# Hybrid decoder step: attention loop written out, second branch's inputs loaded early, first norm and first feed-forward tile reordered

## What is computed

```python
u_a = (jax.nn.silu(rg) * rn) @ w_pa
u_b = fox_o.reshape(b, t, FOX_W) @ w_pb
merged = jax.nn.sigmoid(ga) * u_a + jax.nn.sigmoid(gb) * u_b
mix = merged @ w_o
...
h = layer_norm(ALPHA * x + mix, ln1_w, ln1_b)
u, g = h @ w_up, h @ w_gate                    # D_FF = 2816
a = gelu(causal_conv3(u) + conv_b) * g
y = layer_norm(ALPHA * h + a @ w_down, ln2_w, ln2_b)
```

## Time and profile before

| | us |
|---|---|
| runs shown | 2134.36, 2138.0, 2139.96; median 2138.0 |
| profiled execution | 2139.22, of which the span between first and last instruction is 2137.5 |
| TensorE busy | 1989.5 (93% of the span) |
| VectorE, ScalarE, GpSimd busy | 1159.1, 648.8, 218.8 |
| granted TensorE clock | 0.97 on average |

### The profile page before, as it was taken

How to read it: one execution, slowest core, us unless ns; L and a number is a source line. 1 busy time by engine, 2 the same in 40 slices (tenths; PEclk the granted TensorE clock), 3 DMA queues, 4 the chain that set the end, 5 groups by cost and what they waited for, 6 DMA issues and landing times.

```text
span 2137.5 us, 39105 instructions
## 1 busy us (share of the span) xinstructions
PE 1989.5 (93%) x14335; PEld 1861.5 (87%) x14335; DVE 1159.1 (54%) x1771; ACT 648.8 (30%) x1179; POOL 218.8 (10%) x253
## 2 busy tenths in 40 slices
PE   7898998899999899989898898799999999999996
PEld 5796896798898798878798897799999999999996
DVE  4554454977867867885424856533322333233348
ACT  4444343134133223213401103434301322132224
POOL 1000000020020020020000101300000000100004
PEclk9999999999999999989999999899999999999999
DMA  4211101787987878886732310111111111111144
GB/s 126 63 32 50 40 21 51 233 311 245 310 281 262 301 264 298 278 308 231 252 94 89 106 49 11 40 49 40 50 49 50 40 48 43 54 42 49 43 142 131
DMA packets 151682, 276.50 MB, mean 129 GB/s; under 512 B 19042, under 2 KB 57951, under 8 KB 151543
## 3 DMA queue, kind: packets, MB, share of 16 engines
...
q0 software_dynamic: 23232, 82.80, 13.0%
...
## 4 chain that ended last, share of the span: by engine, by line
PE 44%; DVE 5%; DMA 1%; issue 1%; ACT 1%; SPq 0%; DVEq 0%; ACTq 0%
PE bank L121 40%; PE bank L1670 3%; DVE x_lo L1898 1%; DMA gated_raw<-gated_t_scratch 1%; DVE chunk_tmp L1827 1%; DVE chunk_tmp L1829 0%; DVE z L1895 0%; DVE moving_lo L1833 0%; DVE merged_hi L1831 0%; PE banks L1628 0%; DVE w_lo L1968 0%; DMA tail_raw<-in_w_down_dram 0%; DVE y L1944 0%; DMA z<-fox_t_scratch 0%; PE banks L1656 0%
## 5 line engine op out<-in xcount | busy, mean ns | idle before, releaser
L121 PE MATMUL bank<-x_hi,w_hi 128*128 128x344 f32 (+1 forms) x1944 | 641.5, 330 | 44.4 <-DVE x_lo L1898 15.1
L121 PE MATMUL bank<-x_lo,w_hi 128*128 128x344 f32 (+1 forms) x1944 | 631.6, 325 | 0.0
L121 PE MATMUL bank<-x_hi,w_lo 128*128 128x344 f32 (+1 forms) x1944 | 631.3, 325 | 0.0
L121 PEld LDWEIGHTS bank<-x_hi,w_hi 128*128 128x128 f32 (+1 forms) x1944 | 372.4, 192 | 61.6 <-issue 48.6
L121 PEld LDWEIGHTS bank<-x_lo,w_hi 128*128 128x128 f32 (+1 forms) x1944 | 372.5, 192 | 1.6
L121 PEld LDWEIGHTS bank<-x_hi,w_lo 128*128 128x128 f32 (+1 forms) x1944 | 372.1, 191 | 1.7
L97 ACT ACTIVATE w_hi<-w_raw 128x1024 fp32r<-128x1024 f32 (+3 forms) x139 | 142.1, 1022 | 453.7 <-PE bank L121 419.5
L121 PE MATMUL bank<-moving_hi,w_hi 128*128 128x344 f32 x744 | 227.0, 327 | 13.7 <-DVE moving_hi L1806 7.0
L121 PE MATMUL bank<-moving_lo,w_hi 128*128 128x344 f32 x744 | 237.6, 319 | 0.0
L104 DVE TENSOR_TENSOR w_lo<-w_raw,w_hi 128x1024 fp32r<-128x1024 f32 (+3 forms) x139 | 164.4, 1182 | 103.2 <-ACT w_hi L97 101.4
L121 PE MATMUL bank<-moving_hi,w_lo 128*128 128x344 f32 x648 | 208.1, 321 | 0.0
...
## 6 DMA issues: line engine op xcount, KB each, us to landing
...
```

What stands on the lines that cost most here:

```text
L121: mm = pe.matmul(g.bank[n][0:m, 0:TC], w[slot][:, k, 0:m], x[:, k, chunk(n)], start=(k == 0 and i == 0), stop=(k == kt - 1 and i == 2))
```

## The change

Three things are changed.

**Attention loop.** On all five engines the loop of two in `fox` is written out as straight code.

```diff
             @block.tensor
             def _(pe):
-                with pe.Fori(0, NIT) as it:
+                for it in range(NIT):
                     for u in range(2):
```

```diff
-        raw = [g_raw[:, n, :] for n in range(KD)] + [z[:, KB + n, :] for n in range(KB)]
+        fo_slot = [z[:, KB + n, :] for n in range(KB)]
+        raw = [g_raw[:, n, :] for n in range(KD)] + [gate[0][:], gate[1][:], stage[0][:, 0:T], fo_slot[3]]
...
+                for b in (0, 1):
+                    for n in range(NCH):
+                        sp.wait_ge(g.bank_free[n], JA + KD - 1 - b + 1)
+                    load_raw(KD + b)
+                load_raw(KD + 2)
                 sp.wait_ge(g.mm_chunk, NCH * (RING + JB))
-                for n in range(KD, KD + KB):
-                    load_raw(n)
+                load_raw(KD + 3)
                 for i in range(KD, 2 * KD):
+                    if i < KD + 2:
+                        sp.wait_ge(s_lo, i + 1)
                     load_gate(i)
...
                 split_hi(g, act, job(JB, JB % 2, 0), KB)
+                act.wait_ge(g.mm_chunk, NCH * (RING + JB))
                 for n in range(KD, KD + KB):
                     raw_hi(n)
...
-                dve.memset(zsum[:], 0.0).then_inc(z_part, 1)
...
                 merged(LAST, 1)
+                dve.memset(zsum[:], 0.0).then_inc(z_part, 1)
                 dve.wait_ge(s_lo, KD + KB)
```

```diff
+                        up_and_gate(1, f0, ju)
                         for k in range(NCH):
-                            pool.wait_ge(normed, (k + 1) * KD)
+                            pool.wait_ge(h_full, (k + 1) * KD)
+                            pool.wait_ge(h_lo, (k + 1) * KD)
                             for t in range(KD):
-                                ins = pool.tensor_scalar(acc[:, t, chunk(k)], z[:, t, chunk(k)], ln_cols[:, 1, t:t + 1], ALPHA, ALU.add, ALU.mult)
+                                ins = pool.tensor_scalar(acc[:, t, chunk(k)], z[:, t, chunk(k)], ALPHA, None, ALU.mult)
...
+                pe.wait_ge(centred, NCH)
+                pe.wait_ge(root, 2)
+                for n in range(NCH):
+                    for (j, slot), dst in ((up_job, bank[n]), (gate_job, gate_bank[n])):
+                        pe.wait_ge(g.w_split, RING + j + 1)
+                        pe.wait_ge(g.bank_free[n], ju + 1)
+                        for k in range(KD):
+                            pe.wait_ge(h_lo, n * KD + k + 1)
+                            for q, (w, x) in enumerate(((g.w_hi, g.xh), (g.w_hi, g.xl), (g.w_lo, g.xh))):
+                                mm = pe.matmul(dst[:, 0:TC], w[slot][:, k, :], x[:, k, chunk(n)],
+                                               start=(k == 0 and q == 0), stop=(k == KD - 1 and q == 2))
+                        mm.then_inc(g.mm_chunk, 1)
+                pe.wait_ge(z_part, 2)
+                pe.wait_ge(g.bank_free[NCH - 1], ju + 2)
+                pe.transpose(bank[3][0:NS + 2, 0:P], up[:, SEQ:SEQ + NS + 2], g.ident[:]).then_inc(cr_t, 1)
...
+                    with pe.Fori(0 if f0 else 1, n) as i:
+                        product(g, pe, job(i * 2 + ju, ju % 2, 0), g.xh, g.xl)
                         product(g, pe, job(i * 2 + ju, ju % 2, 1), g.xh, g.xl)
...
+                        act.activation(z[:, k, chunk(n)], z[:, k, chunk(n)], ACT.Identity, scale=ln_cols[:, 0, k:k + 1], bias=ln_cols[:, 1, k:k + 1]).then_inc(h_full, 1)
+                        act.wait_ge(h_full, n * KD + k + 1)
+                        act.activation(g.xh[:, k, chunk(n)], z[:, k, chunk(n)], ACT.Copy).then_inc(h_hi, 1)
                 act.wait_ge(ln_land, 32)
                 squares(0)
+                split_hi(g, act, job(JF, JF % 2, 1))
                 squares(1, range(0, 3))
...
+                        if first:
+                            act.wait_ge(g.mm_chunk, NCH * (RING + ju) + 2 * NCH - 1)
                         split_hi(g, act, job(i * 2 + ju, ju % 2, 2))
...
+                    if s == 0:
+                        tile(0, True)
+                    with act.Fori(1 if s == 0 else 0, n) as i:
+                        tile(i, False)
...
+                centre(0)
+                split_lo(g, dve, job(JF, JF % 2, 1))
+                centre(1)
+                centre(2)
+                dve.memset(up[:, 0:2], 0.0).then_inc(z_part, 1)
...
+                invert(0)
+                for k in range(KD):
+                    scale(0, k)
+                for n in range(NCH):
+                    if n < NCH - 1:
+                        invert(n + 1)
                     for k in range(KD):
+                        h_low(n, k)
+                        if n < NCH - 1:
+                            scale(n + 1, k)
...
+                            if first:
+                                dve.wait_ge(g.mm_chunk, NCH * (RING + ju) + 2 * k + 2)
+                            else:
+                                chunk_ready(g, dve, i * 2 + ju + 1, k)
```

56 lines of the change are left out of this document (30 added, 26 removed).

## The result

The changed kernel takes 2113.28 us (median of 4 runs, 2112.10 to 2114.90), the kernel before beside it 2138.98. The ratio is 0.9884, with a 95% interval of 0.9869 to 0.9900: 24.8 us less (21.4 to 28.0). A second set of runs gave 0.9891 (0.9873 to 0.9909). The forecast was 19.0 us less, 2119, in a range of 2112 to 2127. So the time lies in the range, near its lower end, and the direction is right; but 19.0 lies outside the interval of the measured gain, and some 4 to 6 us were not in the sum. The profiled execution took 2114.34 us with a span of 2112.4; the spans differ by 25.1 us.

The account below looks back on a forecast made before the run. TensorE, busy for 93% of the span, was taken as the bound, so time could come only from its standstills or lower clock. 7.5 + 4.5 + 7.0 = 19.0 us less than 2138.0 gave 2119, range 2112 to 2127.

Parts of the forecast that it names:

- Part A: Attention loop written out: TensorE's stall at the loop's jump and the half clock behind it go; 7.5 us, 4.3 to 9.5.
- The term for the rest: Attention: registers that computed semaphore values go too, in engines handing over work in softmax steps; 0.5 us, bounded 0 to 1.5.
- Part B: Raw inputs of the JB jobs: three loads come early, so merging starts sooner after the JA jobs; 4.5 us, 3.3 to 4.9.
- Part C: Norm and feed-forward tile 0: a loss at the start, a gain at the end, tile 1 starting earlier; 7.0 us, 1.0 to 9.
- The split's loss: Norm's start: VectorE stops behind the first centring for tile 0's gate weights, so ScalarE starts `h_high` 4.1 us late.
- The middle: Norm's 24 tiles, now two ScalarE passes each, 1.10 us a tile; it ends 1.8 us later than before.
- give-backs: Before tile 1: GpSimd's `acc` chunk beside the convolution costs 1.1 us, TensorE's possible start at the lower clock 1.0.
- the third rival: All three changed places reach the good ends of their bounds: 23.4 us less, 2114.6; chance 0.12 with beyond.
- The first rival: Norm: ScalarE's second pass becomes the bound, `x_lo` ends some 6 us later, 2125; chance 0.18.
- the second (a wait that remains): Attention: the 5.16 us idle time remains, so writing out the loop gives 0 to 1 us, 2126; chance 0.08.
- the fourth (straight code starves TensorE): Attention: fetching falls behind once in each pair, four stalls make 25 us, 2145, slower; chance 0.03.
- The fifth: ScalarE's second pass bounds the norm and the attention loop gives nothing, together: 2132; chance 0.03.

Follow-up runs that it names:

- the old arithmetic: Changed kernel with the norm's former arithmetic: one ScalarE pass for the high half, weight and bias on VectorE; median 2114.07 us, ratio 0.9890 to the kernel before.

## Why the prediction was right, and where it was short

**Part A: the mechanism right, two terms too small.** The forecast was 7.5 us (4.3 to 9.5); over all traces the stage takes 239.8 us with all loops and 229.8 without, 10.0 less, outside that range. That the 5.16 us were TensorE's own jump is shown: the idle time was there, 5.26 us, with every other engine written out, and went with TensorE's loop alone. That the sequencer fetches code in this time is the reading of the prediction; the row says only issue. The term for the jump was 7.0, chosen between the idle time and the pairs' difference of 8.0; pair 2 fell by 8.2. The term for the rest was 0.5, for registers, but pair 3 fell from 77.1 to 75.2, which I had taken for its plain length. With all loops the half clock in the softmax of pairs 2 and 3 was longer, which I had not priced. By the pairs above, 3.4 us of it in each pair are worth 2 to 3 us, most of the 3.7 that went with the other engines' loops. This part of the cause is argued from the traces and not isolated.

One row was misread, without harm: the 0.11 us of the earlier trace rows between two feed-forward tiles is the transpose of L1644, and TensorE has no idle time there. So the short loop's jump costs nothing that can be seen. And retention does have a standstill that is put down to issue, the one of 3.1 us in the earlier trace rows, so straight code is not free of them; it is there in all fourteen traces (2.1 to 3.5 us) and changes nothing in the comparison.

The Trainium skill, "Runtime: NRT & Kernel Launch", section Instruction fetch mechanics, says that a taken branch out of the fetched window stalls; this case's rows agree, with 4.6 to 5.5 us of idle time in the five traces with TensorE's loop, and none behind the short loop's jump. In the first trace the idle time above the usual 0.7 is 4.5 of the 10.0 us.

**Part B: right, and a little too small.** Merging starts 7.2 to 7.3 us after the JA jobs in seven of the nine traces with this part and 6.8 in the other two, where it was 12.0: 4.8 us earlier, or 5.2, for a forecast 4.9. Over all traces the stage is 159.4 us without and 154.0 with the part: 5.3, above the range's 4.9. I had taken off 0.4 for chunks at the lower clock, whatever the old kernel did there. But the old kernel had the half clock at the start of merging too (0.59), and its stretch, by the stretch view, was over 10 us long against 3.4 or 6.8. Where it is 3.4, the stage takes 153.1 to 153.7 us (four traces), where it is 6.8, 154.2 to 154.9 (the other five): so the clock gave something back instead of taking it. (The bound of 1.6 us for what could come back is not what its own numbers give, two chunks at 3.4 - 2.3 = 1.1 each, so 2.2; nothing hung on it.)

**Part C: right, with errors that cancel.** The forecast was 7.0, the stage gave 6.8 in the first pair of traces and 7.2 over all. The split's loss was to be 4.1 us; 3.9 was read, and 4.2 came back when it was moved. The period of ScalarE was 1.09 us for a forecast 1.10. The middle ended 1.3 us later for a forecast 1.8. From the last low half to tile 1 it took 8.2 us instead of 17.9 (the 18.1 of the working had the old start 0.2 late); forecast 7.2 and up to two give-backs. These were sized wrong one by one: GpSimd beside the convolution cost 0.6 us and not 1.1 (from the convolution's first step to the first gate product 4.7 us, in the next tile 4.1); the last up chunk is copied 1.1 us behind the last low half and not 0.5, because TensorE was still busy with the products before it; and the start of tile 1 at the lower clock cost 1.6, not 1.0. VectorE's row of the convolution beside GpSimd, which takes 1.28 us in the next tile:

```profile
1343.37 1.52 DVE L1967 SCALAR_TENSOR_TENSOR stage<-stage,conv_cols_tile 128x1024 f32<-128x1024 f32 x1 [2.64 <-ACT stage L1783]
```

The Trainium skill's rule of a locked port pair ("SBUF — State Buffer", section SBUF: two separate sides), which I had weighed at 4 us, did not hold as a full lock in these rows: VectorE's low halves went from 0.52 to 0.78 us in seven of 24, GpSimd's instructions took 1.14 us (median) instead of 0.80 (their form had changed too), and three of the convolution's four steps grew by 0.2 us each.

**What was in no term.** 4.7 us of retention and 2.9 us lost at the start. The second is scatter. Of the first, the means over all traces leave 3.6 us that may belong to the change, and that stays open.

**How much was luck.** The measured time is the one of the third rival (23.4 us less, 2114.6), to which I gave 0.12 with all beyond, and not the forecast's own 2119. The three stages give 10.0 + 5.3 + 7.2 = 22.5 us, which would be 2115.5. So the range would have held by the three parts alone. But parts A and B both lie above their own bounds, and part C is not at its upper end, as that rival had it: the time came out there for other reasons than the rival's.

The first rival (ScalarE's second pass as the bound) is out by the period and by the old arithmetic; the second (a wait that remains) by the two kernels on TensorE's loop; the fourth (straight code starves TensorE) by pairs of 75 us without an issue wait at their start. The fifth, the first and second together, falls with them.
